# A decoder trunk of two layers: the arms of TensorE's overflow branch exchanged

## What is computed

```python
def reference(x, ...):
    for i in range(DEPTH):                      # DEPTH = 2
        mix = moba_attention(...) if i % 2 == 0 else nsa_attention(...)
        x = layer_norm(DEEPNORM_ALPHA * x + mix, ln_g[i, 0], ln_b[i, 0])
        ffn = grouped_moe(x, router_w, router_b, moe_w_gate[i], moe_w_up[i], moe_w_down[i])
        x = layer_norm(DEEPNORM_ALPHA * x + ffn, ln_g[i, 1], ln_b[i, 1])
    return x

# grouped_moe: for each expert e and the tokens xt that chose it
hid = jax.nn.silu(xt @ w_gate[e]) * (xt @ w_up[e])
out[tokens] += (hid @ w_down[e]) * weight
```

## Time and profile before

| | before |
|---|---|
| median of three runs | 1202.12 us (1201.18 to 1203.4) |
| the profiled execution | 1202.28 us, of which 1200.5 us is the span of its instructions |
| TensorE busy | 1021.0 us, 85% of the span |
| TensorE's instructions | 7688 MATMUL and 7688 LDWEIGHTS |
| VectorE, ScalarE, GpSimd busy | 334.0, 185.3, 43.1 us |
| mean granted TensorE clock | 0.928 |
| DMA | 449.05 MB, mean 374 GB/s |
| the chain that ended last | TensorE 50%, DMA 44%, VectorE 3% |

### The profile page before, as it was taken

The page is one execution under the profiler, slowest core; times in us unless marked ns, Lnnn a source line. Parts: engine busy times, 40 slices in busy tenths (PEclk is TensorE's granted clock), DMA queues, the critical chain, the costliest instruction groups (busy, mean ns, idle before and its releaser), DMA issues.

```text
span 1200.5 us, 18510 instructions
## 1 busy us (share of the span) xinstructions
PE 1021.0 (85%) x7688; PEld 565.4 (47%) x7688; DVE 334.0 (28%) x902; ACT 185.3 (15%) x474; POOL 43.1 (4%) x109
## 2 busy tenths in 40 slices
PE   9999999986689966678899999999876889766865
PEld 7576544443343433343598655444533534433432
DVE  2435521321111111111563785303211111111112
ACT  1024210110010100000321553110100010100002
POOL 1001010000000000000100110100000000000000
PEclk9999999998789987788999999999978899978889
DMA  9937899999999999999993609999999999999995
GB/s 349 371 141 263 317 395 414 429 425 428 427 427 428 427 427 427 426 427 423 377 362 119 250 2 349 386 413 424 427 427 427 428 427 429 427 428 425 427 425 211
DMA packets 59348, 449.05 MB, mean 374 GB/s; under 512 B 4580, under 2 KB 10981, under 8 KB 32637
## 3 DMA queue, kind: packets, MB, share of 16 engines
q1 hardware_dynamic: 57248, 442.52, 89.7%
q0 software_dynamic: 1680, 4.88, 1.2%
q10 hardware_dynamic: 332, 0.42, 0.1%
HBM read 446.72 MB, written 1.07 MB: 373 GB/s over the span
## 4 chain that ended last, share of the span: by engine, by line
PE 50%; DMA 44%; DVE 3%; ACT 1%; issue 1%; SPq 1%; DVEq 0%
DMA ring<-in_moe_w_gate 17%; DMA ring<-in_moe_w_up 16%; PE bank L1137 14%; DMA ring<-in_moe_w_down 11%; PE bank L890 5%; PE bank L990 5%; PE bank L1219 4%; PE bank L919 3%; PE bank L1101 3%; PE bank L1195 2%; PE bank L1373 2%; PE bank L1468 1%; PE bank L1234 1%; PE bank L1399 1%; PE bank L1237 1%; PE bank L961 1%
## 5 line engine op out<-in xcount | busy, mean ns | idle before, releaser
L1137 PE MATMUL bank<-ring,work 128*32 128x256 f32 (+1 forms) x2656 | 328.6, 482 | 103.8 <-DMA ring<-in_moe_w_up 38.5
L1137 PEld LDWEIGHTS bank<-ring,work 128*32 128x32 f32 (+1 forms) x2656 | 152.3, 133 | 237.4 <-issue 208.5
L1838 DVE TENSOR_TENSOR work<-work,bank 128x256 f32<-128x256 f32 (+1 forms) x32 | 15.6, 488 | 514.8 <-PE bank L1137 514.8
L1219 PE MATMUL bank<-ring,work 128*32 128x512 f32 x576 | 96.7, 642 | 15.2 <-DMA bias<-in_moe_w_down 8.2
L1137 PE MATMUL bank<-softmax_area,work 128*32 128x256 f32 (+1 forms) x352 | 64.2, 489 | 28.1 <-DMA ring<-in_moe_w_gate 19.4
L1851 DVE TENSOR_TENSOR xs<-xs,bank 128x512 f32<-128x512 f32 x112 | 71.2, 684 | 50.3 <-PE bank L1237 32.0
L1137 PE MATMUL bank<-bias,work 128*32 128x256 f32 (+1 forms) x384 | 76.8, 491 | 0.0
L1101 PE MATMUL bank<-work,acc 128*128 128x128 f32 (+1 forms) x448 | 75.5, 323 | 0.0
L1101 PEld LDWEIGHTS bank<-work,acc 128*128 128x128 f32 x448 | 66.0, 191 | 16.6 <-issue 11.5
L2255 ACT COPY work<-bank 128x256 f32<-128x256 f32 (+1 forms) x32 | 13.6, 426 | 312.5 <-PE bank L1171 246.9
L990 PE MATMUL bank<-ring,work 128*128 128x512 f32 x128 | 59.3, 604 | 0.5 <-DVE work L1612 0.5
(11 more groups left out here) (308 smaller groups left out, 1203.9 us busy)
## 6 DMA issues: line engine op xcount, KB each, us to landing
ring<-in_moe_w_gate SPq DMA_DIRECT2D x44, 2048.0 KB, 29.9
ring<-in_moe_w_up SPq DMA_DIRECT2D x40, 2048.0 KB, 28.9
ring<-in_moe_w_down SPq DMA_DIRECT2D x36, 2048.0 KB, 29.3
softmax_area<-in_moe_w_down SPq DMA_DIRECT2D x8, 2048.0 KB, 26.1
ring<-in_moe_w_down SPq DMA_DIRECT2D x12, 1024.0 KB, 8.7
ring<-in_moe_w_gate SPq DMA_DIRECT2D x12, 1024.0 KB, 9.3
bias<-in_moe_w_gate SPq DMA_DIRECT2D x6, 2048.0 KB, 33.6
softmax_area<-in_moe_w_up SPq DMA_DIRECT2D x6, 2048.0 KB, 27.6
```

Of the source, the lines that this page charges most:

```text
L1137: last = mm(bank[2 + k][row:row + cap, 0:width], xgT_of(group_of[i])[:, t, at + e * cap:at + (e + 1) * cap], w[e](t)[:, part * width:(part ...
L1219: last = mm(bank[5][row:row + CAP_NARROW, :], hidT_narrow[:, m, CAP_NARROW * e:CAP_NARROW * (e + 1)], w[e](m)[:, n * 512:(n + 1) * 512], s ...
```

## The change

In `last_pair_and_overflow` the condition is turned round and the two arms are exchanged: now the arm without overflow follows the branch, and the arm with the last pair and the overflow's loop stands behind it. The instructions within the arms are the same. Only TensorE's program is changed; the branches of the other engines stay.

```diff
             def last_pair_and_overflow(l):
-                with pe.If(flag[l] > 0):
+                with pe.If(flag[l] < 1):
+                    last_pair(l)
+                with pe.Else():
                     last_pair(l)
                     pe.wait_ge(acc_added[l], 4 * PAIRS)
                     tr(bank[6][:, 0:P], ident, ident).then_inc(ov_pe[l], 1)
...
                             pe.wait_ge(ov_dve[l], n + 6)
                             tr(bank[6][:, 0:P], ident, ident).then_inc(ov_pe[l], 1)
-                with pe.Else():
-                    last_pair(l)
                 if l + 1 < LAYERS:
                     keep_warm(3)
```

## The result

The changed kernel takes 1207.14 us in the median of five runs (1205.89 to 1207.89), the kernel before 1202.12 us in the runs beside it: a ratio of 1.0044, 95% interval 1.0033 to 1.0055, or 4.0 to 6.6 us more. Forecast were 1207.5 us, +5.2. The profiled execution of after has a span of 1205.3 us, 4.8 longer.

The account below looks back on a forecast made before the run. Expert stages were taken as bound by weight transfers, layer-1 attention by compute. Removed branch 0, layer 1 0, jump +3.6 and clock +1.6 gave +5.2 on 1202.3, so 1207.5 us; range 1204.0 to 1209.8 (81 in 100).

Parts of the forecast that it names:

- The bound: Expert stages end on weight transfers, so time lost before DMA waits is absorbed; layer-1 attention is compute-bound and passes TensorE delays through.
- Removed, 0: Taken branch ahead of the last pair goes: spread starts 2.0 us earlier in layer 0, 2.6 in layer 1; worth 0.
- the stall of 1.0 us: Behind layer 0's gate matmuls, the next instruction block's late arrival costs 1.0 us; it was to go with the branch.
- The jump, +3.6: Layer 0's new jump ends at 587.9 us; warming matmuls queue behind it, so transposes start at 590.6, not 587.01.
- second stall: None expected at the merge behind both arms, which stays at its address, about 180 instructions ahead of a block's end.
- The clock, +1.6: After layer 0's jump, TensorE's 4.2 us idle lowers its clock: +1.6 us, bounds 0 and 2.6.
- The sum: 0 (layer 0, removed) + 0 (layer 1) + 3.6 (jump) + 1.6 (clock) = +5.2 us.
- Layer 1's jump, 0: Layer 1's jump of 6.3 us ends at 1195.8, before the end at 1200.5, with only the final DRAIN behind: 0.
- The drained queue: Rival: the fetch begins only when TensorE's queue has drained; transposes 2.0 to 2.7 us late, 1204.3 to 1206.6; 15 in 100.
- The cheap jump: Rival: the jump is cheap, being unconditional or its target already there; 1202.3 us, no change; 12 in 100.
- The faster rival: Rival: the kernel gets faster, a layer's last loads coming on one late DMA engine; 3 in 100.

Follow-up runs that it names:

- x1_layer0_only: The arms are exchanged in layer 0 only and layer 1 keeps the old order; 1207.66 against 1201.51 us for the kernel before, ratio 1.0052.
- x7_else_last_pair: Changed kernel with the second arm cut to the last pair and one transpose, some 440 instructions; its single execution took 1206.46 us.
- x9_loads_held: Changed kernel with SP's first load of layer 1, and all behind it, held until layer 0's first tokens are normed; one execution took 1210.94 us.
- x8_more_warm_before_jump: Changed kernel with sixteen warming MATMULs queued ahead of the jump and none behind it; 1205.09 against 1201.92 us for the kernel before, ratio 1.0021.
- x6_short_else: Changed kernel with the second arm cut to one transpose, so the jump goes a few instructions ahead; 1200.75 against 1201.92 us for the kernel before, ratio 0.9986.
- x3_no_branch: Changed kernel with no flag branch and no overflow program on TensorE, the last pair run straight through; 1201.10 against 1201.51 us for the kernel before, ratio 0.9993.
- x4_warm_before_jump: Changed kernel with the three warming matmuls moved to the end of each arm, ahead of the jump; 1203.31 against 1201.51 us for the kernel before, ratio 1.0013.
- x10_branch_in_pair14: Kernel before, with the branch moved between pair 14's gate and up products; 1201.74 against 1201.65 us for the kernel before, ratio 0.9997.

## Why the prediction was right

**The bound.** The time fell where it was said: what moved before a DMA wait moved the end by 1.2 us at most by the medians, and of the shift of 5.59 us at layer 1's start 4.85 went through (the rest below). Layer 0's exchange alone gave the whole loss, layer 1's nothing that can be told.

**Removed, 0.** Right within the 1.2 us of the medians. In detail it was partly wrong: I said the gate would start as before and the stall of 1.0 us go, so that the down weights' wait would grow from 0.78 to 2 us. It is 0.86 us. The weights themselves came about 1 us earlier (gate 559.22 for 560.29, last down 579.02 for 580.04), which I had excluded and which no run explains. The gate, after a wait of 3.05 us, ran partly at the lower level and took 5.0 us, which ate the stall's 1.0, and the up products still started without a wait. I had the clock's loss for layer 1's gate in the text and not for layer 0's.

**The jump, +3.6.** Right. It was taken at 581.8 + 6.1 = 587.9 in the old trace's time; measured, it starts with the last spread (580.8 and 580.78), takes 6.37 us, and the first matmul behind it starts 6.45 us after the spread. At full clock the transposes would have come 6.45 + 2.6 - 5.21 = 3.8 us late. No second stall came behind the merge, as forecast.

**The clock, +1.6.** Too small. The six MATMULs took 5.28 us from first start to the transposes and not 2.6, so 2.7 us were lost, a little over the upper bound of 2.6 that I had given. I had read the loss from stretches in which the clock came back before the work was done; here the low level lasted for all six. `x1_layer0_only` has the same (5.47 us), but in `x7_else_last_pair`, with an idle of 4.50 ahead, they took 4.54 (granted clock 0.63), a loss of 1.7: a matter of the execution, and my 1.6 was at the low end of what these three profiles show.

**The sum.** The terms as measured give 3.8 + 2.7 = +6.5 us at the transposes, against 5.2 forecast and 5.0 measured in the median. The difference of 1.5 us has two parts in the profile of after. Layer 0 ended 1.0 us earlier than in the earlier trace rows, 0.7 of it already at the changed branch (its first record starts at 550.4, in the earlier trace rows at 551.1). And the last 0.7 was paid out of the first wait for weights in layer 1's experts, before and after:

```profile
864.03 3.64 PE L1219 MATMUL bank<-ring,work 128*32 128x512 f32 x32
871.41 6.60 PE L1137 MATMUL bank<-ring,work 128*32 128x256 f32 x64 [3.74 <-DMA ring<-in_moe_w_gate]
```

```profile
869.62 3.64 PE L1219 MATMUL bank<-ring,work 128*32 128x512 f32 x32
876.26 5.27 PE L1137 MATMUL bank<-ring,work 128*32 128x256 f32 x64 [3.00 <-DMA ring<-in_moe_w_gate]
```

Up to there TensorE is 5.59 us late throughout, behind that wait 4.85, and the span is 4.8 longer. I had said that layer 1's loads would move with attention; these moved by 0.7 us less. Why the weights came sooner in both places is open: it may be the scatter between executions, or the removed branch's 0.4 to 1.2 us. `x1_layer0_only` had 6.1 us in the median. So the sum's closeness, 5.2 against 5.0, is in part luck: the clock's term was 1.1 us too small in this execution, and what nobody had forecast made up for it.

**Layer 1's jump, 0.** Right, and it is shorter than I took it: 3.5 in place of 6.3 us, like layer 0's with no weights streaming (3.29 us, `x9_loads_held`).

**The rivals.** The drained queue falls by `x8_more_warm_before_jump`: the packet starts 3.5 us after the jump's start and 3.5 us before the queue has drained. The packets that had followed the queue's end by 0.0 and 0.7 us stand as well at 3.8 and 3.4 us after their branches' starts (551.1 and 1157.6). The cheap jump is what happens where the target is near: 0.18 us in `x6_short_else`. The 0.05 us that I gave as the bound for a near jump was an estimate, and no run shows it. Where the target isn't near, the record has 3.3 to 6.45 us, and 6.41 already over 440 instructions (`x7_else_last_pair`); from which distance on isn't measured. The faster rival has nothing for it.

## What to carry to other kernels

In this kernel a far jump is paid by its place, by the medians 5.0 us with the one in after between layer 0's last spread and layer 1's first transposes, and 0.4 and 1.2 us (`x3_no_branch`, `x6_short_else`) with those of before ahead of the last pairs' waits: put it where a wait of its length follows on that engine, not between the last result of one stage and the first product of the next. The likely arm placed first still ends in a far jump if the other arm is long (6.37 us over some 1430 instructions, 6.41 over some 440). Work that is only there to keep the clock up belongs ahead of such a jump, in the queue, where it ran during the fetch (2.84 us at a granted clock of 1.00, `x4_warm_before_jump`); behind it, it was late and ran at the low clock itself (5.49 us at 0.50, after).

## What the runs showed of the hardware that I had not expected

- The price of a far jump on TensorE depended on the DMA traffic: 5.9 to 6.45 us while weights stream, 3.3 to 3.7 us where none do. A packet of q8 starts 3.4 to 3.9 us after the jump's start in the first case and 0.9 to 1.3 us in the second. In the same place and with the same target distance it is 6.37 us (after, at 580.8) and 3.29 us (`x9_loads_held`, at 581.2).
- Distance had two prices in the sizes tried, while weights stream: 0.18 us for a few instructions (`x6_short_else`), 6.4 us for some 440 (`x7_else_last_pair`) as for some 1430 (after).
- The sequencer ran only so far ahead: with sixteen MATMULs and their weight loads more, the jump is reached at 583.4 and not with the spread at 581.5 (`x8_more_warm_before_jump`).
- A move of the branch into pair 14's wait of 6 us didn't take its cost away altogether: the block behind the target came late too, 0.53 us of idle within the work (`x10_branch_in_pair14`). Whether that reached the end isn't shown.
